# PEER gates scattered into a matrix in DRAM, the dense pass moved to the first pair of blocks, and 64 more gathered rows beside layer 0's second up pass

## What is computed

```python
def peer_ffn(h, wq, subkeys, u_tab, v_tab):      # per block of 128 tokens, hb [128, 1024]
    q = (hb @ wq).reshape(128, 8, 2, 128)
    s = jnp.einsum('thpd,hpnd->thpn', q, subkeys)
    top_s, top_i = lax.top_k(s, 16)
    cand_s = (top_s[:, :, 0, :, None] + top_s[:, :, 1, None, :]).reshape(128, 8, 256)
    cand_i = (top_i[:, :, 0, :, None] * 128 + top_i[:, :, 1, None, :]).reshape(128, 8, 256)
    best_s, pos = lax.top_k(cand_s, 16)
    idx = jnp.take_along_axis(cand_i, pos, axis=-1)
    g = jax.nn.softmax(best_s, axis=-1)
    a = jax.nn.gelu(jnp.einsum('td,thkd->thk', hb, u_tab[idx]), approximate=False)
    return jnp.einsum('thk,thkd->td', g * a, v_tab[idx])
```

## Time and profile before

| | us |
|---|---|
| median of 3 runs | 5275.13 (5266.3, 5275.13, 5329.87) |
| profiled execution | 5303.6 |
| its span | 5301.9 |
| granted TensorE clock, mean | 0.944 of full speed |

### The profile page before, as it was taken

One profiled execution on the slowest core, in us unless ns is written; L12 is line 12 of the kernel. 1 busy time (PEld: TensorE's weight loads), 2 busy tenths in 40 slices (PEclk: granted clock), 3 DMA queues, 4 the chain that ended last, 5 costly groups with the idle time before them and its releaser, 6 DMA issues.

```text
span 5301.9 us, 75651 instructions
## 1 busy us (share of the span) xinstructions
PE 4666.2 (88%) x25798; PEld 3895.4 (73%) x25798; DVE 3121.5 (59%) x6247; ACT 1525.4 (29%) x2757; POOL 1827.7 (34%) x1918
## 2 busy tenths in 40 slices
PE   8889899999788876898998987799999948999998
PEld 6569788999777765555555665588899947778886
DVE  2673646666356656454554655646576736667777
ACT  2333422534212233000000023334253425222322
POOL 1111210000456557666666411113000041666652
PEclk9989999999889989999999998799999969999999
DMA  4331115656479863888998942212365722889997
GB/s 150 112 104 54 31 72 177 223 176 211 145 259 321 304 219 123 316 320 317 335 334 330 371 173 79 79 62 66 131 215 177 226 77 76 318 321 339 359 356 267
DMA packets 316699, 1103.74 MB, mean 208 GB/s; under 512 B 59392, under 2 KB 108672, under 8 KB 267872
## 3 DMA queue, kind: packets, MB, share of 16 engines
q1 hardware_dynamic: 165024, 648.09, 35.1%
q0 software_dynamic: 151488, 453.35, 23.9%
HBM read 1037.13 MB, written 62.03 MB: 207 GB/s over the span
## 4 chain that ended last, share of the span: by engine, by line
PE 69%; issue 9%; another core or an unknown queue 7%; DVE 7%; ACT 4%; POOL 2%; POOLq 1%; DMA 1%; ACTq 0%; DVEq 0%; PEldq 0%; SPq 0%
PE PS L1277 16%; PE PS L1352 14%; PE PS L1361 7%; PE PS L1376 6%; PE PS L1222 5%; PE PS L939 3%; PE PS L937 3%; PE PS L1259 3%; PE PS L1180 3%; PE PS L1019 2%; POOL arena L671 1%; PE PS L998 1%; DVE PS L2471 1%; PE PS L1076 1%
## 5 line engine op out<-in xcount | busy, mean ns | idle before, releaser
L1277 PE MATMUL PS<-hS,wS 128*128 128x256 f32 x7680 | 974.5, 289 | 92.4 <-ACT wS L1677 69.1
L1277 PEld LDWEIGHTS PS<-hS,wS 128*128 128x128 f32 x7680 | 954.2, 196 | 109.4 <-issue 80.4
L671 POOL DMA_INDIRECT arena<-hx,arena x768 | 788.5, 1027 | 630.6 <-POOLq L406 333.0
L1352 PE MATMUL PS<-hS,ring 128*128 128x256 f32 x4096 | 954.4, 384 | 51.5 <-issue 41.4
L1352 PEld LDWEIGHTS PS<-hS,ring 128*128 128x128 f32 x4096 | 786.4, 192 | 233.2 <-issue 119.4
L2501 DVE TENSOR_TENSOR wS<-ring,wS 128x1024 fp32r<-128x1024 f32 x320 | 392.0, 1225 | 469.0 <-ACT wS L1677 382.3
L677 POOL DMA_INDIRECT arena<-in_experts,arena x465 | 480.7, 1034 | 515.1 <-DVE PS L2471 392.5
L2471 DVE SCALAR_TENSOR_TENSOR PS<-arena,PS 128x1024 f32<-128x1024 f32 x462 | 593.4, 1284 | 26.3 <-DMA arena<-in_experts,arena 13.2
L1361 PE MATMUL PS<-ring,arena 128*128 128x512 f32 x1024 | 488.1, 622 | 61.2 <-DVE arena L2638 53.8
L1795 ACT ACTIVATE arena<-PS 128x256 f32<-128x256 f32 x256 | 97.3, 384 | 1280.7 <-PE PS L1352 776.9
L2638 DVE TENSOR_TENSOR arena<-arena 128x256 f32<-128x256 f32 x256 | 108.8, 425 | 533.8 <-ACT arena L1795 354.6
(11 more groups left out here) (331 smaller groups left out, 6299.4 us busy)
## 6 DMA issues: line engine op xcount, KB each, us to landing
ring<-in_experts SPq DMA_DIRECT2D x256, 1024.0 KB
ring<-in_experts SPq DMA_DIRECT2D x384, 512.0 KB
ring<-in_wcat SPq DMA_DIRECT2D x80, 1024.0 KB
hx<-arena SPq DMA_DIRECT2D x384, 128.0 KB
ring<-in_wq SPq DMA_DIRECT2D x40, 1024.0 KB
arena<-in_rpb POOLq DMA_DIRECT2D x96, 128.0 KB, 2.6
arena<-hx,arena POOLq DMA_INDIRECT x768
arena<-xs POOLq DMA_DIRECT2D x20, 512.0 KB, 5.6
```

Source lines behind the costliest of these rows:

```text
L671: pool.indirect_dma_start(out=aX[n][:, k:k + 1], out_offset=None, in_=src, in_offset=bass.IndirectOffsetOnAxis(ap=at[:, k:k + 1], axis=0)) ...
L1277: mm = pe.matmul(bank[6 + c % 2][:, 0:PASS], u[:, k, :], hS[:, h, k, :], start=(part == 0 and k == 0), stop=(part == 2 and k == KD - 1))
L1352: mm = pe.matmul(bank[c % 2][:, 0:PASS], u[:, k, :], hS[:, 0, k, :].bitcast(F32), start=(k == 0), stop=(k == KD - 1))
```

## The change

The pairs change roles. The dense pass works on the first pair (layer 0: blocks 0, 1; layer 1: 2, 3), the gathered passes on the later ones (layer 0: 2, 3, then 4, 5; layer 1: 4, 5). The first queries are of the dense pair, whose normed inputs go to DRAM (`hd`) and come back before the dense pass. The norms of the next pair stand among these queries.

`retrieve` of the dense pair runs at 2.0 steps per chunk over the first pass's 32 chunks before the next queries (before: 1.25 over 44). Its picks give pick numbers eD and gates gD (`chosen`), and GpSimd adds the gates to a matrix `gd` in DRAM by 256 indirect DMAs of 128 elements of 4 bytes: in layer 0 224 in the first pass and 32 at the start of the second, in layer 1 all in the only pass. `gd` is set to zero by 16 DMAs of 1 MB in each layer's attention. In the dense pass SP loads a 128 KB tile of gates beside each 1 MB of experts. The gate stage is gone. Of the rows, 192 instead of 128 are taken beside layer 0's second pass, and 320 instead of 384 beside its dense pass; 40 activation gathers stand ahead of the first row of each dense pass.

```diff
 def gathered_passes(layer):
-    return range(first_block(layer), NB - 2, 2)
+    return range(first_block(layer) + 2, NB, 2)
...
+def queries_at(layer, f):
+    return 8 if first_pass(layer, f) else 4
...
+def row_start(layer):
+    return 2 if beside_products(layer) else 9
...
             def dense(l):
...
+                for sl in range(SLOTS):
+                    sp.wait_ge(s["slot_free"], base + sl - SLOTS + 1)
+                    load(0, sl)
+                for tb in range(2):
+                    sp.wait_ge(scattered[tb], 16 * P * (l + 1))
+                for sl in range(SLOTS):
+                    gates(0, sl)
+                with sp.Fori(1, PK // SLOTS) as i:
+                    for sl in range(SLOTS):
+                        sp.wait_ge(s["down_done"], i * SLOTS + (l * PK + sl - SLOTS + 1))
+                        load(i, sl)
+                        gates(i, sl)
...
+                for i in range(16):
+                    sp.wait_ge(s["exp_done"], 1 + at_unit + 2 * i)
+                    sp.dma_start(gd[i * size:(i + 1) * size, :].rearrange("(p t) o -> p (t o)", p=64),
+                                 k8[64:128, 0:size // 64]).then_inc(s["zero_out"], 16)
...
+                def scatter(heads):
+                    for h in heads:
+                        for tb in range(2):
+                            if h:
+                                pool.wait_ge(scattered[tb], 16 * (P * l + TOPK * h))
+                            for k in range(TOPK * h, TOPK * (h + 1)):
+                                pool.indirect_dma_start(out=gd, out_offset=bass.IndirectOffsetOnAxis(ap=eD[:, tb, k:k + 1], axis=0),
+                                                        in_=gD[:, tb, k:k + 1], in_offset=None, compute_op=ALU.add
+                                                        ).then_inc(scattered[tb], 16)
...
+                    if first_pass(l, f):
...
+                        pool.wait_ge(s["gates_ready"], l + 1)
+                        scatter(range(HEADS if l + 1 == DEPTH else HEADS - 1))
                     else:
...
+                        scatter([HEADS - 1])
                         rows0 = t.get("rows", 0)
                         take_activations(3, f0, range(32))
...
-                        for r in range(P):
+                        for r in range(P + FEW):
...
-                head = 16 if not early else 0
+                head = 40
...
-                queries(hP)
+                queries(hD, 2)
...
-                            some_steps(own, c, 1.25)
+                            some_steps(own, c, 2.0)
...
-                        dve.tensor_tensor(gel[2 + c % 2], gel[c % 2], G[:, c, :], ALU.mult).then_inc(s["gfull"], 1)
+                    dve.wait_ge(g_in[c % SLOTS], 16 * (l * PK // SLOTS + c // SLOTS + 1))
+                    dve.tensor_tensor(gel[2 + c % 2], gel[c % 2], Gb[:, c % SLOTS, :], ALU.mult).then_inc(s["gfull"], 1)
```

More of the change, by code:

```diff
@@ L117, in rows_due @@
         for c in range(PK):
-            have = sum(not f or f + lead <= c for f in free)
-            at += min(step, have / 2 + 0.5) if have else 0
+            at += min(step, buffers / 2 + 0.5) if c >= start else 0
             due.append(min(total, int(at)) if c < PK - 1 else total)
@@ L125, in row_plan @@
         step += 1 / 64
[L126 to L135, removed]
+    return rows_due(step), [r % buffers for r in range(total)]
 class Chain:
@@ L398, in build @@
         v_in = [sem(f"v_in{i}") for i in range(NV)]
+        scattered = [sem(f"scattered{tb}") for tb in range(2)]
+        g_in = [sem(f"g_in{i}") for i in range(SLOTS)]
         w_ready = [sem(f"w_ready{i}") for i in range(SLOTS)]
@@ new lines, in group @@
+                def group(i, first, last):
+                    for sl in range(SLOTS):
+                        if sl < SLOTS - 1:
+                            up(i, sl + 1, sl + 1)
+                        elif not last:
+                            up(i + 1, 0, 0)
+                        down(i, sl, sl, first and sl == 0, last and sl == SLOTS - 1)
+                pe.wait_ge(s["h_in"], 16 * (ps_ + 1))
+                up(0, 0, 0)
+                group(0, True, False)
+                with pe.Fori(1, PK // SLOTS - 1) as i:
+                    group(i, False, False)
@@ L1408, in _ @@
+                group(PK // SLOTS - 1, False, True)
+                if not split_rows(l):
+                    pe.wait_ge(s["down_done"], cbase + PK)
+                    with pe.Fori(0, PK // 16) as i:
+                        pe.nop().then_inc(s["slot_free"], 16)
+                t["tiles"] += PK
+                t["dense"] = ps_ + 1
+                end(f"gemm{l}")
         @block.scalar
@@ new lines, in _, with v_high @@
+                ps_ = t.get("dense", 0)
+                cb = ps_ * PK
+                t0 = t["tiles"]
+                sb_ = sum(split_rows(m) for m in range(l)) * PK
+                def v_high(i, c, first=False):
+                    sl = c % SLOTS
+                    act.wait_ge(w_ready[sl], (i + c // SLOTS) * 16 + 16 * (t0 // SLOTS + 1))
+                    if not (first and c < 2):
+                        act.wait_ge(s["down_done"], i * SLOTS + (cb + c - 1))
+                    act.activation(wS[:, 2 * (c % 2), :], ring[:, sl, D:2 * D], ACT.Copy).then_inc(s["v_hi"], 1)
```

787 lines of the change are left out of this document (335 added, 452 removed).

## The result

The changed kernel takes 5685.9 us (median of 4, 5676.0 to 5692.6) beside 5302.5 for the kernel before: ratio 1.072, interval 1.063 to 1.082, so 7% slower. The prediction was 5182 with a range up to 5420. The profiled execution took 5692.6 us, 389 more than that of before.

The account below looks back on a forecast made before the run. The prediction took TensorE, busy 88%, to carry the time. Gate-stage savings of −109 and −165 us and added costs summed to −93, giving 5182 us against the 5275.1 median; own range 5120 to 5245, full range 5010 to 5420.

Parts of the forecast that it names:

- C: Layer 1's only gathered pass: its 256 scatters end at 4329, after the products at 4275; about +50 us.
- D: Layer 0's first pass: its 224 scatters end at 1324, before the pass end at 1330; 0 us.
- rival 4: Scatters in both layers: an accumulating scatter takes 2.5 us, twice a gather; total 5697 us, chance 0.05.
- F: Layer 0's second pass: 32 scatters ahead of its gathers +28 us, 64 more rows +28; together +56.
- A and B: Gate stages of layers 0 and 1 removed, about 12 us left for each hand-over: −109 and −165 us.
- Q: Queries in the first passes: 46 back-to-back scatters per layer hold up TensorE, +15 us a layer, +30.
- rival 3: First passes: back-to-back scatters hold up the other engines as gather bursts did; +211 us, 5486, chance 0.18.
- freeze: Layer 1's gate stage, layer 0's second pass: back-to-back indirect DMAs hold up TensorE's semaphores; 33 instructions lost 20.3 us.
- E: Denser retrieval in the first passes, 2.0 steps per chunk, VectorE 93% busy: +10 us a layer, +20.
- G: Layer 0's dense pass: 40 gathers ahead of the first row +25 us, less transfer −10; +15.
- H: Layer 1's dense pass: 512 GpSimd instructions instead of 448, and 16.8 MB of gate tiles; +10 us, bounds 0 and +47.
- Rival 1: Scatters are free: they run at 1.25 us, freeze nothing, denser retrieval fits; −221 us, 5054, chance 0.22.

Follow-up runs that it names:

- the paced kernels: Kernel before with gate-stage gathers spaced by semaphores: 5290.6 us (5300 kind), 4933.6 (4922 kind); also the first 32 of layer 0's second pass: 5254.9 and 5260.2, 4933.9.

## Why the prediction was wrong

- **Which step failed.** C and D, "the price of a scatter is no row's; the gather is the nearest": I paced scatters at 1.25 to 1.56 us. They run at (4719 − 4186)/256 = 2.08 and (1470 − 997)/224 = 2.11: 1.86 beside the queries and alone, 2.3 beside the products (122 in 283 us). The start was right (gates ready 108 us into layer 1's pass, predicted 118), and so was the rest of C and D: what waits behind the scatters, and that the products beside them go on. With 2.08 in my own sum, C is 3944 + 256 × 2.08 − 4275 = 201 instead of 50 (measured: a wait of 190, some 9 of it hand-over, behind products that took 8 more), and D is 989 + 224 × 2.1 − 1330 = 129 instead of 0 (measured: a wait of 118 more, behind products that took 16 more). That is 280 us of the error of 482 (−93 forecast, +389 measured), and turns the forecast by itself into slower.
- The bound that I gave this price, 1.56 at most, came from a gather on both sides. Nothing in the trace excluded a dearer one; rival 4 said 2.5 and 5697 us, with a chance of 0.05. It was the right mechanism, 0.4 us too dear, and its total of 5697 beside the measured 5686 is luck: terms that I had too small made up for it.
- **F, second pass of layer 0**, was +56 and is +149. By stretches: the part before the queries is 31 us shorter, since no gathers go out there, the queries are 49 longer, since they do here, and the stretch of rows is 130 longer. So the scatters ahead of the pass cost 18 up to the end of the queries, beside the +28 that I gave them, and the rest is the rows, +28 forecast. These 64 rows were priced by the mean loss per instruction (0.42 us); moving them back gave 112 us in that pass. The step should have compared two rates: rows wanted per chunk against what GpSimd can issue, 2.5 us for a row and its gather.
- **A and B** were right: the first dense products start 8.6 us (layer 0) and, with half of the scatters, 8.8 us (layer 1) behind the last up product, where I left 12.
- **Q and rival 3.** Beside scatters nothing was held up: TensorE worked 62.70 of the 63 us of layer 0's queries and 280.42 of the 283 behind layer 1's. The freeze is real, as the paced kernels show, but not at a scatter's cadence of 1.85 us. What the change did was to move its burst of 32 gathers, out of the chunks (52 us for 83) into the queries (111 for 62).
- **E** was 10 per layer: the two passes' products took 16 and 8 us more. The sum was right.
- **G** was +15 and is +34, inside its bounds of −40 and +40 (+42 on the other kind, 919 for 877 us).
- **H** was +10 and is +113 here, but +4 on the other kind of chip (795 us for the 791 of the paced kernels of before). Some 45 us of it lie in its first 100, where 40 gathers go out in a row (TensorE 54.03 us busy, before 99.39). Pacing them gave back 15 of these. ScalarE's waits that the profile can't place are 210 us in the pass, before 93, and none on the other kind; the variant with one head's scatters has them too, so they are not the scatters'. What makes them stays open.
- **The zeroing** was 0 and is some 25 in layer 1. Two slices of DMA rate do not show that a transfer costs nothing there.
- Rival 1's time, 5054, is what the scatters would have to cost nothing for; the kernel with one head's scatters is 1% slower than before, so even this wasn't within reach: on the 5300 kind the rows and layer 1's dense pass ate the gate stages' 274 us.

The changed kernel's gate stages were worth what they looked: their work went to an engine that was idle, but in a form which takes that engine 2.08 us for 128 numbers, 512 times: 1065 us, for gate stages of 285.

## What to carry to other kernels

Before work is moved to an idle engine, count the instructions and ask what one costs in exactly this form: an accumulating indirect DMA is not a gather, and where the trace has none of the kind, the upper bound has to lie well above the nearest row (here the measured 2.08 was 1.7 times the gather's 1.25), not at that row beside a busy neighbour. A stream that rises in a stage is to be judged by the two rates, wanted and issued, and not by what it cost on average when it was not yet the bound. Bursts of GpSimd's indirect DMAs are worth pacing by a semaphore of the engine that they run beside: it gave 0.7 to 1.4% here on one kind of chip and cost 0.2% on the other. And a stage is compared from the same event to the same event: cut at round numbers, layer 1's dense pass seemed 10 us better than it was.

## What the runs showed of the hardware

- An indirect DMA of 128 elements of 4 bytes takes GpSimd 1.10 us as a scatter that writes and 1.78 us as one that adds (means over 512; 0.97 and 1.55 where nothing else runs), with 0.30 us between two.
- Chips differ by 8% on the same kernel: 4922 and 5302 to 5339 us for before, 5282 and 5686 to 5689 for after. The waits that the profile calls "remote" are there on the one kind and absent on the other. ScalarE's, in the changed kernel on the 5300 kind (in its trace on the other kind there is none):

```profile
ACT arena L1758 <- remote: 569.9, 51, 48.7
ACT arena L1684 <- remote: 205.0, 18, 19.2
ACT wS L1751 <- remote: 101.9, 15, 27.5
```

- In layer 1's gate stage and in the first part of layer 0's second pass these waits go with bursts of indirect DMAs at 1.25 us and not with scatters at 1.85: pacing the bursts removed them there. Why a burst should delay a semaphore on one chip and not on another was not found.
- Most of these waits lie elsewhere, before the gelu of the dense passes above all, and pacing those bursts did not take them away there: 358.3 us in the kernel before, 541.6 to 588.7 in the paced kernels on the 5300 kind. That bursts cause these too is not shown.
- The granted clock is lower where TensorE idles, and its matmuls take longer: the same 2248 matmuls took 359.49 us in a stretch that is 98% busy and 401.59 in one that is 77% busy, at mean granted clocks of 1.00 and 0.89. In the 125 and 190 us in which it does nothing the clock is 0.52 and 0.51.
